# Ten pairs of weight blocks of the first projection by seven block products instead of eight

## The reference

```python
def short_conv_fourier_mixer(h, w_in, conv_w, w_out):      # h = rms_norm(x, norm_even)
    proj = h @ w_in                                        # 1024 x 1024 by 1024 x 3072
    a_x, a_b, a_c, a_z, b_u, b_z = jnp.split(proj, [...], axis=-1)      # 512 wide each
    y_a = a_b * centred_depthwise_conv(a_c * a_x, conv_w) * jax.nn.silu(a_z)
    f = jnp.fft.fft2(b_u by groups of 128, axes=(1, 3), norm="ortho").real
    y_b = f * jax.nn.silu(b_z)
    return jnp.concatenate([y_a, y_b], axis=-1) @ w_out
```

## Time and profile before

| | us |
|---|---|
| median of 3 runs | 1753.91 (1752.42 to 1754.14) |
| the profiled execution, its own time | 1752.93 |
| its span in the profile | 1751.1 |
| TensorE busy | 1710.2 (98%) |
| VectorE busy | 1051.2 (60%) |
| ScalarE busy | 661.6 (38%) |
| GpSimd busy | 452.9 (26%) |

### The profile page before, as it was taken

How to read it: one execution, slowest core, us unless ns; L and a number is a source line. 1 busy time by engine, 2 the same in 40 slices (tenths; PEclk the granted TensorE clock), 3 DMA queues, 4 the chain that set the end, 5 groups by cost and what they waited for, 6 DMA issues and landing times.

```text
span 1751.1 us, 21292 instructions
## 1 busy us (share of the span) xinstructions
PE 1710.2 (98%) x8348; PEld 1416.2 (81%) x8348; DVE 1051.2 (60%) x1281; ACT 661.6 (38%) x845; POOL 452.9 (26%) x288
## 2 busy tenths in 40 slices
PE   7999999999999999999999999999999999999997
PEld 6888888888788888887888877788888788778885
DVE  7342335445677777877775799255655277887223
ACT  6110112225566655576622422110124667682002
POOL 4233233332210110101022332232333222214330
PEclk9999999999999999999999999999999999999999
DMA  5121131132101111011332211112123311336112
GB/s 213 37 72 65 57 132 37 48 136 80 37 1 37 37 37 37 1 37 37 149 123 96 97 36 49 65 38 78 62 91 126 121 49 61 121 133 241 49 36 96
DMA packets 40674, 133.70 MB, mean 76 GB/s; under 512 B 5516, under 2 KB 5900, under 8 KB 40320
## 3 DMA queue, kind: packets, MB, share of 16 engines
q1 hardware_dynamic: 40288, 131.83, 21.1%
q10 hardware_dynamic: 288, 0.52, 0.1%
HBM read 100.61 MB, written 31.59 MB: 75 GB/s over the span
## 4 chain that ended last, share of the span: by engine, by line
PE 87%; DVE 8%; ACT 3%; issue 2%; DMA 0%; SPq 0%; DVEq 0%; ACTq 0%
PE pair L836 49%; PE pair L1055 8%; PE pair L1118 5%; PE aux L1091 4%; PE pair L1104 3%; PE pair L847 2%; PE pair L1399 2%; PE aux L1270 1%; PE pair L855 1%; PE pair L911 1%; PE aux L836 1%; DVE stat_b L2183 1%; PE pair L1384 1%; PE pair L1412 1%; PE aux L1412 1%
## 5 line engine op out<-in xcount | busy, mean ns | idle before, releaser
L737 POOL CAST w_hi<-w_raw 128x1024 fp32r<-128x1024 f32 x106 | 117.6, 1109 | 1111.0 <-issue 1102.5
L836 PE MATMUL pair<-op_hi,w_hi 128*128 128x512 f32 x990 | 307.4, 392 | 0.9 <-DVE op_lo L1954 0.9
L836 PE MATMUL pair<-op_lo,w_hi 128*128 128x512 f32 x990 | 305.0, 389 | 0.0
L836 PE MATMUL pair<-op_hi,w_lo 128*128 128x512 f32 x990 | 304.9, 389 | 0.0
L739 POOL TENSOR_TENSOR w_lo<-w_raw,w_hi 128x1024 fp32r<-128x1024 f32 x106 | 271.9, 2565 | 8.5
L836 PEld LDWEIGHTS pair<-op_hi,w_hi 128*128 128x128 f32 x990 | 185.5, 188 | 41.7 <-issue 2.6
L836 PEld LDWEIGHTS pair<-op_lo,w_hi 128*128 128x128 f32 x990 | 186.0, 188 | 39.0
L836 PEld LDWEIGHTS pair<-op_hi,w_lo 128*128 128x128 f32 x990 | 185.8, 188 | 38.9
L1649 ACT ACTIVATE pt_hi<-pair 128x1024 fp32r<-128x1024 f32 x60 | 61.7, 1028 | 126.7 <-issue 84.6
L1949 DVE TENSOR_TENSOR pt_lo<-pair,pt_hi 128x1024 fp32r<-128x1024 f32 x60 | 73.5, 1225 | 52.4 <-ACT pt_hi L1649 48.9
L1055 PE MATMUL pair<-opb_hi,w_hi 128*128 128x512 f32 x256 | 101.7, 397 | 1.1 <-DVEq L86 0.6
(11 more groups left out here) (403 smaller groups left out, 3076.5 us busy)
## 6 DMA issues: line engine op xcount, KB each, us to landing
w_raw<-weight_units SPq DMA_DIRECT2D x106, 512.0 KB, 3.5
xf<-y_dram SPq DMA_DIRECT2D x12, 512.0 KB, 4.7
x_dram<-xa SPq DMA_DIRECT2D x8, 512.0 KB, 5.9
xc<-x_dram SPq DMA_DIRECT2D x8, 512.0 KB, 7.9
x_dram<-xc SPq DMA_DIRECT2D x8, 512.0 KB, 2.6
y_dram<-y_d SPq DMA_DIRECT2D x8, 512.0 KB, 2.6
mz_dram<-y_d SPq DMA_DIRECT2D x8, 512.0 KB, 2.9
bm_b<-bm_dram SPq DMA_DIRECT2D x8, 512.0 KB, 4.8
```

The lines of the kernel that those rows point to most:

```text
L737: pool.tensor_copy(w_hi[:, u % 2, :], w_raw[:, u % 3, :]).then_inc(w_hi_done, 1)
L836: mm = pe.matmul(acc[:, cols], w, x[:, kx, cols], start=(first and k == 0 and n == 0), stop=(last and k == KT - 1 and n == 2))
```

## The change

Units 0 to 3 stay as they are. Units 4 to 23 become ten pairs (e0, e1). With A11 and A12 the two halves (four blocks) of e0 along the contraction, A21 and A22 those of e1, and B11, B12, B21, B22 the input's quarters (row index: half of the contraction; column index: half of the tokens), the pair's result is made in Winograd's form of Strassen's algorithm:

- weight sums of `[128, 512]`: S1 = A21 + A22, S2 = S1 - A11, S3 = A11 - A21, S4 = A12 - S2
- input combinations, made once: T1 = B12 - B11, T2 = B22 - T1, T3 = B22 - B12, T4 = T2 - B21
- products: P1 = A11 B11, P2 = A12 B21, P5 = S1 T1, P6 = S2 T2, P7 = S3 T3, P3 = S4 B22, P4 = -A22 T4
- results: C11 = P1 + P2, C12 = P1 + P6 + P5 + P3, C22 = P1 + P6 + P7 + P5, C21 = P1 + P6 + P7 + P4

A product is 4 blocks x 3 products x 512 columns, 12 matmuls. P1, P6, P7, P4 add up in one half of `pair[1]`, and ScalarE copies the running sum after P1 and after P6; P5 and P3 share the right half of `pair[0]`, with a copy after P5; P2 has the left half. VectorE adds the rest. It also makes the weight sums (`weight_sum`) and their low parts (`sum_low_part`); GpSimd casts all seven blocks and makes the low parts of the three plain ones. The split weights lie in a ring of four halves. TensorE's order in pair q is P1(q), P4(q-1), P5(q), P6(q), P2(q), P7(q), P3(q), with the transforms in between.

The combinations overwrite parts of `xa`, so x is loaded again for the residual. `w_raw` has four buffers instead of three, the loads of y1 are issued later into other buffers, and some semaphores are joined.

```diff
+def place(q, name):
+    if name == "P4":
+        return 7 * q + (7 if q < PAIRS - 1 else 6)
+    return max(7 * q + AFTER_P1[name], 0)
+def copy_at(q, name):
+    order = ("P1", "P6", "P5") if q % 3 == 1 else ("P1", "P5", "P6")
+    return COPIES + 3 * q + order.index(name) + 1
+def ring(at):
+    return (at + (2 if at >= RING_STEP else 0)) % 4
+        def mixer_of(q):
+            return (q + 2) // 3, (q + 2) % 3
...
@@ SyncE
-                    if u >= 3:
-                        sp.wait_ge(w_split, u - 2)
+                    if FAST <= u - RAW < BASE[1]:
+                        sp.wait_ge(block_made, own_blocks((u - RAW - FAST) // 2, "P4"))
+                    elif u >= RAW:
+                        sp.wait_ge(w_split, plain(u - RAW + 1))
...
+            sp.wait_ge(fft2_done, AB)
+            for k in range(2, THROUGH["y1"]):
+                load_y1(k)
+            weights_to(BASE[1] + 4)
+            sp.wait_ge(product_done, place(PAIRS - 1, "P6") + 1)
+            for k in range(QUAD):
+                sp.dma_start(xa[:, k, :], x_t[k]).then_inc(x_loaded[k], 16)
...
@@ GpSimd: block(q, name)
+                if at < 4:
+                    pool.wait_ge(unit_done, FAST - 1 + half)
+                else:
+                    pool.wait_ge(product_done, at - 1 if at - RING_STEP in (0, 1) else at - 3)
+                pool.tensor_copy(hi, src).then_inc(w_hi_done, 1)
+                if name not in SUM_OF:
+                    pool.wait_ge(w_hi_done, FAST + at + 1)
+                    pool.tensor_tensor(lo, src, hi, ALU.subtract).then_inc(block_made, 1)
...
@@ TensorE: product(q, name)
+                if name in SUM_OF:
+                    pe.wait_ge(sum_low, 4 * q + SUM_OF[name] + 1)
+                else:
+                    pe.wait_ge(block_made, own_blocks(q, name))
+                if name == "P1":
+                    pe.wait_ge(pair_free[1], FAST // 2 + max(q - 1, 0))
+                elif name in ("P5", "P2"):
+                    pe.wait_ge(pair_free[0], FAST // 2 + q)
+                elif name == "P6":
+                    pe.wait_ge(copied, copy_at(q, "P1"))
+                elif name == "P7":
+                    pe.wait_ge(copied, copy_at(q, "P6"))
+                elif name == "P3":
+                    pe.wait_ge(copied, copy_at(q, "P5"))
+                else:
+                    pe.wait_ge(c22_added, q + 1)
...
+                product(q, "P6")
+                product(q, "P2")
+                if turn_of == 1:
+                    fft_channels(j)
+                product(q, "P7")
+                product(q, "P3")
+                if q == 0:
+                    fft_channels(0)
+            product(PAIRS - 1, "P4")
...
@@ ScalarE
+            for k in range(QUAD):
+                link(act.activation(xa[:, k, HALF:S], xa[:, k, HALF:S], ACT.Copy, scale=col("norm_even", k)), copied)
...
+            def copy_p1(q):
+                j, kind = mixer_of(q)
+                if kind == 0:
+                    act.wait_ge(parts_ready, j)
+                elif kind == 1:
+                    act.wait_ge(c22_added, q - 1)
+                else:
+                    act.wait_ge(parts_ready, j + 1)
+                product_copy(q, "P1", first_row[kind][:, 0:HALF])
...
+                if kind == 2:
+                    fourier_gate(j)
+                copy_p5(q)
+                copy_u2(q)
+                if kind == 1:
+                    spectrum(j)
+            for k in range(THROUGH["y1"]):
+                y_hi("y1", k, y1_in[k], op_hi)
+            conv_gate(AB - 1)
+            for k in range(THROUGH["y1"], KT):
+                y_hi("y1", k, y1_in[k], op_hi)
@@ VectorE: 16 gained sums and the first low part, then
+            dve.wait_ge(ax_ready, 1)
+            by_token(ax_sb[:, :], ax_sb[:, :])
+            for n in range(3):
+                weight_sum(0, n)
+            wait_job(dve, 2)
+            link(dve.tensor_tensor(u_pad[:, 1:S + 1], pair[0][:, :], ax_sb[:, :], ALU.mult))
...
+            sum_low_part(0, "P5")
+            sum_low_part(0, "P6")
+            weight_sum(0, 3)
+            convolve(0)
...
+            sum_low_part(0, "P7")
+            dve.wait_ge(bu_ready, 1)
+            fold_parts(0)
+            dve.wait_ge(ax_ready, 2)
+            by_token(sz_b[:, :], sz_b[:, :])
+            signal(scaled_b)
+            for q in range(PAIRS):
+                j, kind = mixer_of(q)
+                sum_low_part(q, "P3")
+                add_c11(q)
+                if q + 1 < PAIRS:
+                    weight_sum(q + 1, 0)
+                    weight_sum(q + 1, 1)
+                add_c22(q)
+                if q + 1 < PAIRS:
+                    sum_low_part(q + 1, "P5")
+                add_c12(q)
+                if q + 1 < PAIRS:
+                    sum_low_part(q + 1, "P6")
+                    weight_sum(q + 1, 2)
+                    weight_sum(q + 1, 3)
+                if kind == 0:
+                    fold_parts(j)
+                    take_c21(q)
+                    if q + 1 < PAIRS:
+                        sum_low_part(q + 1, "P7")
+                elif kind == 1:
+                    link(dve.tensor_tensor(u_pad[:, 1:S + 1], u_pad[:, 1:S + 1], ax_sb[:, :], ALU.mult))
+                    convolve(j)
+                    take_c21(q)
+                    if q + 1 < PAIRS:
+                        sum_low_part(q + 1, "P7")
+                    signal(scaled_b)
+                else:
+                    link(dve.tensor_tensor(cv[:, :], ab_row, cv[:, :], ALU.mult))
+                    if j == AB - 1:
+                        fourier_output(j)
+                        for k in range(QUAD):
+                            low(k, y1_in[k], OP0["y1"])
+                    take_c21(q)
+                    if q + 1 < PAIRS:
+                        sum_low_part(q + 1, "P7")
+                    signal(scaled_a)
+                    if j < AB - 1:
+                        fourier_output(j)
+                    else:
+                        for k in range(QUAD, THROUGH["y1"]):
+                            low(k, y1_in[k], OP0["y1"])
+                    conv_output(j)
```

More of the change, by code:

```diff
@@ L34 @@
 RADIX = 8
+RAW = 4
 HEADS, KV_HEADS = 8, 2
@@ L995, in fft_time, with product @@
                 mm.then_inc(fft2_done, 1)
-            for j in range(AB):
-                for i in range(6):
-                    u = 6 * j + i
-                    if u >= 2:
-                        unit(u, u, op_hi, op_lo, "even", read=even_read if u == BASE[1] - 1 else None)
-                    if i == (3 if j == 0 else 1):
-                        fft_channels(j)
-                    if i == (4 if j == 0 else 2):
-                        fft_time(j)
+            def product(q, name):
+                at = place(q, name)
+                half, col0 = ring(at) // 2, ring(at) % 2 * HALF
+                hi, lo = operands[name]
+                first = name in ("P1", "P2", "P5")
+                if name in SUM_OF:
+                    pe.wait_ge(sum_low, 4 * q + SUM_OF[name] + 1)
[13 more added lines that the diff above has]
+                    pe.wait_ge(c22_added, q + 1)
+                if q == 0 and name in ("P5", "P6", "P7", "P4"):
+                    pe.wait_ge(cmb_low, ("P5", "P6", "P7", "P4").index(name) + 1)
+                for k in range(QUAD):
+                    cols = slice(col0 + k * P, col0 + (k + 1) * P)
+                    for n, (w, x) in enumerate(((w_hi, hi), (w_hi, lo), (w_lo, hi))):
+                        mm = pe.matmul(accumulator(q, name), w[:, half, cols], x[:, k, :],
+                                       start=(first and k == 0 and n == 0),
+                                       stop=(k == QUAD - 1 and n == 2), skip_group_check=(not first))
+                mm.then_inc(product_done, 1)
@@ new lines, in _ @@
+            for u in range(2, FAST):
+                unit(u, u, op_hi, op_lo, "even")
+            for q in range(PAIRS):
+                j, turn_of = mixer_of(q)
+                product(q, "P1")
+                if q >= 1:
+                    product(q - 1, "P4")
+                product(q, "P5")
+                if q == 1:
+                    fft_time(0)
+                elif q >= 3 and turn_of == 2:
+                    fft_time(j)
+                product(q, "P6")
[4 more added lines that the diff above has]
+                product(q, "P3")
+                if q == 0:
+                    fft_channels(0)
@@ L2001, in _, with gained_sum @@
                                    par[:, PARAMS["norm_in"]:PARAMS["norm_in"] + KT], ALU.mult))
+            def gained_sum(out, k, cols, other, op):
+                link(dve.scalar_tensor_tensor(out=out, in0=xa[:, k, cols], scalar=col("norm_even", k), in1=other,
+                                              op0=ALU.mult, op1=op))
+            left, right = slice(0, HALF), slice(HALF, S)
+            for k in range(QUAD):
+                dve.wait_ge(copied, k + 1)
```

(19 more changed lines are left out.)

391 lines of the change are left out of this document (259 added, 132 removed).

## The result

The changed kernel takes 1759.55 us (median of 7 runs, 1758.28 to 1760.26). The kernel before took 1753.19 beside it (7 runs), so the ratio is 1.0034, 95% interval [1.0022, 1.0046]: slower by 6.4 us, where +4.8 was forecast. The 27.2 us of matmuls that were taken out are all lost again, and some more.

A forecast was written before the change was run, and what follows sets the result against it. TensorE, busy 98%, was taken to bound the kernel. T6 84.0 + E 9.2 + S 1.0 = 94.2 against break-even 89.4 gave +4.8 us, 1758.7 on the median; range 1752.5 to 1767, the forecast's own 1754 to 1764.

The forecast's parts named there:

- T6: Start of product P6 of pair 0, behind VectorE's start-up queue: 82.8 us, counted as 84.0 with 1.2 of half clock.
- S: TensorE's stalls between the start and end of the changed stage: 1 us taken, 0 to 8.5 possible.
- place (b): After P3 of a mixer's second pair: about 15.3 us through ScalarE's copies, against 13.6 + 3.5 until P7.
- place (a): After P3 of a mixer's first pair: 9.4 us of work through fold, against 13.6 until fft_channels; just fits.
- The rival in which VectorE and GpSimd bound every mixer: Handover costs its full length in every mixer: T6 85.5, S 8.5, E 9.5, +14 us, 1768; chance 0.2.
- E: TensorE's stalls at the stage's end, before output high block 7: 8.8 plus 0.4 half clock, 9.2; bounds 7.5 and 10.
- The half clock: Slow matmuls after TensorE's waits: 1.2 us at P6(0), at most double, and 0.4 at the output projection.
- break-even: No time lost or won over the changed stage if T6 + E + S = 324.4 - 235.0 = 89.4 us.
- The difference is carried to the end unchanged: After the third output unit (324.42 before), code is as before and TensorE sets it, so the stage's difference stays.
- The faster rival: Short VectorE and GpSimd instructions slip past each other: 85.7 against 89.4, 3.7 us faster, 1750; chance 0.08.
- costed: Loads of x and y1 costed at nothing, issued over 10 us before need; no wait on weights.

The follow-up runs named there:

- the first experiment: Kernel after, with pair 0's first row in a buffer of its own so the copy of P1(0) waits for nobody: 1756.19 us, ratio 1.0014.
- all three reorderings: Kernel after, with pair 0's first row moved, P3(0)'s low part ahead of fold_parts(0), C21(9) and mixer's outputs ahead of y1's low parts: 1744.46 us, 0.9949.
- the doubled sums: Kernel after, with each weight sum of pairs 1 to 9 made twice by VectorE: 1783.2 us, ratio 1.0167.

## Why the prediction was right, and where its sum was off

**T6.** Forecast 82.8, measured 83.34. Behind it the queue is right by its steps: the gained sums end at 51.5 with GpSimd's share (forecast 51.5), the convolution starts at 67.1 (65.4 without holds), fold_parts at 76.4 (74.3 without), and its end is at 82.6 (82.0 with the 1.4 of holds). The holds, the time in which GpSimd keeps VectorE from its operands, were 2.0 us instead of 1.4. That the wait is `parts_ready` was shown by the first experiment. P1(0) waited 1.3 (forecast 1.4), and P5(0) started at 65.7 (about 65).

**S.** Forecast 1, bounds 0 to 8.5, measured 0.1: from P6(0) on, 67 products (182.4), four mixers' transforms (28.1) and 2.6 of half clock lead to 296.46, and P4(9) starts at 296.52. But there is little slack behind that zero. At place (b) ScalarE's copy ends at 290.83 and P7(9) starts at 291.05, 0.2 us later; at place (a) the parts of the second mixer end at 134.87, 1.7 us before the transform. 2.9 us more a pair on VectorE became 15.8 us of waits in three mixers, and longer holds by GpSimd 11.4 (three waits for parts, three for copies). The rival in which VectorE and GpSimd bound every mixer was wrong for this kernel, yet it is what both these experiments show. S = 8.5 needed nearly all of GpSimd's 3.7 to 4.3 us in each tight stretch to fall on VectorE. The trace has 2.5 us at place (a) (12.0 us from the end of P3(1) to the parts, 9.4 counted without GpSimd) and 1.7 at place (b) (17.0 from the end of P3(8) to ScalarE's copies, 15.3 counted). "Fully blocks" of the Trainium skill, "SBUF — State Buffer", section "Who interferes with whom", speaks of one instruction against another, and there the trace agrees: VectorE's subtraction at 61.36 takes 3.25 us for 2.29 while GpSimd's runs to 62.47. It does not say how often the two meet, and the rival took it to mean always.

**E.** Forecast 8.8 and 0.4. Block 7 started at 314.58, where it would have stood at 296.52 + 9.07 = 305.59: 9.0. The wait of 7.0 is there as forecast, the second one is 0.7 instead of 2.

**The half clock: the term that was mis-sized.** The forecast had 1.2 at P6(0) ("at most double") and 0.4 at the output projection, taken from the slow matmuls at the kernel's start, read as six. The trace of before has two more there, in TensorE's timeline:

```profile
10.98 1.05 PE L836 MATMUL pair<-op_hi,w_hi 128*128 128x512 f32 x2
11.83 0.66 PE L836 MATMUL pair<-op_lo,w_hi 128*128 128x512 f32 x2
```

That is eight matmuls in 3.55 us, some 1.7 us lost: the term was misread by half a microsecond, and read rightly it would still have been too small. Measured were 2.6 (half clock from 83.34 to 88.60, 12 matmuls and the start of the next) and 3.0 (from 314.58 to about 320.7). These 4.0 us are the difference in the stage, for the errors of the other terms (T6 +0.5, S -0.9, E +0.2) all but cancel: 83.3 + 2.6 + 0.1 + 9.0 + 3.0 = 98.0 against the break-even 89.4, +8.6, where the chain shows +8.7 and the forecast had +4.8. Filling the gaps gave 5.9 us back, 5.3 of the two half clocks' 5.6 and a T6 of 0.6 less. That the start of the kernel showed fewer slow matmuls than these places is a fact of the trace; why was not found.

**"The difference is carried to the end unchanged"** was off by 1.9 us in the two profiled executions, in the other direction. From the third unit to the end, and the span give 1426.7 us; after took 1424.8, the first experiment 1427.5, all three reorderings 1427.6, the doubled sums 1427.0. The code there is the same. Half of the largest difference, 2.8 us, could be located: in an attention head TensorE waits 2.5 us for VectorE in each kernel. TensorE's timeline and the clock behind the wait, in the kernel after:

```profile
837.25 0.39 PE L1302 MATMUL pair<-pt_hi,v_all 128*128 128x256 f32 x1 [2.52 <-DVE pt_lo L2197]
```

```profile
838.00:840.00 2.00, 2.00 (x19) 2.00 (x19) 1.93 (x3) 0.53 (x2) 0.00 (x0) 1.00 0.00 0
```

and the same place in the kernel with all three reorderings:

```profile
818.98 0.38 PE L1306 MATMUL pair<-pt_hi,v_all 128*128 128x256 f32 x1 [2.51 <-DVE pt_lo L2201]
```

```profile
819.00:822.00 3.00, 3.00 (x15) 3.00 (x16) 2.90 (x4) 1.52 (x2) 0.00 (x0) 0.54 0.00 0
```

The same wait, the same matmuls; once the clock stays, once it falls, and VectorE's next steps come 1.5 us later. Between before and after this place is equal. Their difference is 0.8 us in small steps over the attention and 1.1 in the mLSTM scan, where short VectorE instructions next to GpSimd's take 0.16 us in that of after and up to 0.92 in that of before. All this is no larger than the scatter between runs of one kernel (1758.3 to 1760.3 for after), so no run shows that it belongs to the change. The forecast came nearer in the total (+4.8 to +6.4) than in the stage (+4.8 to +8.7) by luck: it had the half clock too small and nothing for these later 1.9 us.

The faster rival is refuted for this kernel: the holds did not shrink. Weights, x and y1 were on time as costed: TensorE waited for none of them.

## What to carry to other kernels

Taking out matmuls pays only what the engine that feeds TensorE can follow; here the whole 27 us were spent at the two ends of the stage, and moving a buffer and two groups of instructions in VectorE's queue turned +6.4 into about -9 us. When a forecast puts TensorE to a wait of some microseconds, add to each the slow matmuls behind it; behind waits of 7 us and more they cost 1.9 to 3 us here. And a stage that shows no stall may have no time to spare: ask for the distance between the last release and the start, not only for the waits.

## What the runs showed of the hardware

In the kernel after, the matmuls behind the 12.2 us wait ran at half clock for 5.3 us, which cost 2.6; those behind the waits of 7.0 and 0.7 us ran at half clock until 6.1 us after the second of them, which cost 3.0. A longer wait was not followed by a longer stretch: with the low parts given back to GpSimd, P6(0) waited 19.5 us, and its matmuls were slow for 4.0 us, which cost 1.9.

The same wait was not always followed by the same clock either. Behind the 3.6 us ahead of P5(0), all twelve matmuls were 0.43 us apart in the kernel after (granted clock 0.50 from 65 to 71 us), the first eight in the experiment with the row of its own, and in the one with another order at the end the first six were at full clock and the last six at half. Waits of 2 to 3.3 us were followed by either clock, as the two pairs of 2.5 and 3.27 us ahead of the same matmuls show.

One such place moved the time by 1.5 us. The 42 runs of the kernel before that were made beside the experiments fall into two groups about as far apart: 17 took 1752.1 to 1752.9 us, at a mean granted clock of 0.997 to 0.998, and 22 took 1754.0 to 1754.6, at 0.996 to 0.997, with three between them. That a place of this kind is the cause was not shown; only one execution of the kernel before has a trace.

VectorE and GpSimd slow each other both ways when they meet: in the kernel with all three reorderings GpSimd's subtraction took 3.18 us for 1.3, while VectorE's 512-element instructions next to it took 1.3 for 0.69.
